# A decoder layer (mLSTM and SwiGLU) in float32: order of small steps at the seams between stages changed, on five engines

## The chip, the cores and the metric

One core of a Trainium2 chip runs the whole program. The metric is the device time of that core in microseconds. Its engines are TensorE (PE in the profile), VectorE (DVE), ScalarE (ACT), GpSimd (POOL) and SyncE (SP); each runs its own instruction list in order, and they meet only through semaphores.

## The reference

One layer over 2048 tokens of width 1024. The input is normalised, goes through a chunkwise mLSTM with 8 heads, is added back, normalised again, and goes through a gated feed-forward layer of width 2816:

```python
u = rmsnorm(h, mix_norm_g)
h = h + mlstm_mixer(u, w_in, b_if, norm_g, w_out)
u = rmsnorm(h, ffn_norm_g)
h = h + (jax.nn.silu(u @ w_gate) * (u @ w_up)) @ w_down
```

The mixer projects `u` to queries, keys, values, an output gate and two scalar gates per head; scans over chunks with a decayed state per head; normalises each head; multiplies with the sigmoid of the output gate; and projects with `w_out`.

## The kernel before

The tokens are done in two halves (`h` = 0, 1) of 1024, each half as 8 tiles (or chunks) of 128. Every large product is done as three passes of the matrix engine: each float32 operand is split into a high part, which ScalarE makes with a copy (`op_hi`, `proj_hi`, `feed_hi`, `drain_hi`), and a low part, which VectorE makes as the difference (`op_lo`, `proj_lo`, `feed_low`, `drain_lo`). The large products also use a seven-product (Strassen) scheme over 2x2 blocks, so that sums of blocks are needed: of the rows of `x` (`sum_early` on VectorE, `sum_late` with `sum_t3` and `sum_t4` on GpSimd) and of the weights (`proj_sums`, `feed_sums`, `drain_sum`).

A half goes through these stages:

1. Opening. `norm1_sum` (ScalarE) and `norm1_rows` (VectorE) normalise a tile of rows; TensorE transposes it (`turn_unit`, 16 units a stage), and the result is split (`op_hi`, `op_lo`). The units are transposed between the first projections (`project(n, k0, k1)`), each `project` needing its weights and, the first of them, the first four `op_lo`.
2. Projections, 84 units of 12 matmuls; the results are put together in `pkept` and stored (`store_block`, GpSimd). The last block but for one, `store_block(11, 1)`, waits for the last `sigmoid` on ScalarE.
3. Chunks `c` = 0 to 7: `spread`, `scores`, `weights`, `state_sums`, `outputs`, `turn_v`, `turn_heads`, and the output projection `out_tile(c, jj, k0, k1)` for the two halves `jj` of its columns, one chunk (`jj` = 0) or three (`jj` = 1) later. The values of a chunk lie in `v1[c % 2]`, whose last column holds ones; a memset on GpSimd writes it once per half, and `state_sums` waits for it through `ones_set`. `wo` is split into high and low parts in steps `split_out(jj, k)` on both engines. `add_out` adds an output tile into `res`, which a DMA has filled with rows of `x`.
4. The second turn: `norm2_sum`, `norm2_rows`, `sum_early(st + 1, p)`, `turn_unit(st + 1, n)`, between the last `out_tile` and the first `feed` units of the feed-forward layer. `feed` unit 0 waits for four `op_lo`.
5. `feed`, 11 groups of 14 units, then `drain`, 77 units `e` of 12 matmuls, which multiply with `w_down`. SyncE loads `g_in` for each `e` (four buffers) and, at the units in `LOAD_AT`, blocks of `w_down`. GpSimd loads `res` again, when the drains in `RES_AT` are done. In the last drains of the first half the opening of the second is begun: `ROWS_AT` and `SUMS_AT` say after which `e` a tile is normalised or summed, `TURN_AT` = 69 where four units are transposed.

The order on every engine is written out by hand, and an instruction that waits holds all behind it. The waits in `turn_unit` on `op_lo_done` say when a bank of PSUM is free again: unit `n` needs `op_lo` of unit `n - 2`, counted in order.

## Time and profile before

| | |
|---|---|
| median of 3 runs | 2154.61 us (2154.42 to 2155.74) |
| time of the profiled execution | 2154.42 us |
| its span in the trace | 2152.8 us |
| TensorE busy | 2121.9 us, 99% |
| VectorE busy | 1425.7 us, 66% |
| ScalarE busy | 939.2 us, 44% |
| GpSimd busy | 250.1 us, 12% |
| mean granted clock of TensorE | 0.999 |

The span goes from the first to the last record of the trace; the device time has 1.6 us around it. Lines such as L2139 are lines of the kernel; helpers such as `turn_four` (L1891) or `op_lo` (L1309) have one line for many places, so that a place is found by its time.

### The profile page before, as it was taken

To read this page: it belongs to the slowest core of one execution; us is meant where nothing else is said; L and a number is where in the kernel's file an instruction comes from. 1 tells how busy PE (TensorE), PEld (TensorE's weight loads), DVE (VectorE), ACT (ScalarE), POOL (GpSimd) and SP (SyncE) were. 2 spreads that over 40 slices of the span, in tenths; PEclk is the share of its full clock that TensorE was granted. 3 is DMA by queue.
4 is the path that set the end of the run, shared out by engine and by line. 5 is a ranking of instruction groups with operands and counts; after the bars stand their busy time and mean duration, and the time that the engine had idled before them with its cause. 6 is when DMAs were issued, how large, how long until landed. Compare 5 with 4: busy or idle time off the path is not lost.

```text
span 2152.8 us, 29471 instructions
## 1 busy us (share of the span) xinstructions
PE 2121.9 (99%) x10424; PEld 1762.6 (82%) x10440; DVE 1425.7 (66%) x2274; ACT 939.2 (44%) x1686; POOL 250.1 (12%) x357
## 2 busy tenths in 40 slices
PE   6999999999999999999999999999999999999999
PEld 5888888888888888888878888888888888888887
DVE  8765476787566565679677644767866657556764
ACT  5433674453333333345444347544533333334443
POOL 3211100021001010100121111001110101001000
PEclk9999999999999999999999999999999999999999
DMA  4333373223322334773414334632233232357443
GB/s 148 110 110 113 109 272 121 84 69 106 105 96 97 117 102 150 270 249 118 152 64 142 118 94 147 233 119 89 68 103 109 97 117 96 105 190 250 152 134 107
DMA packets 200288, 281.56 MB, mean 131 GB/s; under 512 B 12912, under 2 KB 131696, under 8 KB 200176
## 3 DMA queue, kind: packets, MB, share of 16 engines
q1 hardware_dynamic: 171696, 183.07, 26.5%
q0 software_dynamic: 28480, 97.02, 12.9%
q8 instruction: 68, 1.11, 0.2%
q14 instruction: 44, 0.36, 0.1%
HBM read 197.73 MB, written 82.31 MB: 130 GB/s over the span
## 4 chain that ended last, share of the span: by engine, by line
PE 94%; DVE 3%; DMA 1%; ACT 1%; issue 1%; POOL 0%; SPq 0%; DVEq 0%; POOLq 0%
PE ps L2247 13%; PE ps L2250 13%; PE ps L2249 13%; PE ps L1971 7%; PE ps L1975 7%; PE ps L1973 7%; PE ps L2295 6%; PE ps L2297 6%; PE ps L2299 6%; PE ps L1884 3%; PE ps L1886 3%; PE ps L1885 3%; PE ps L1891 2%; PE ps L2157 1%; DMA res<-in_x_dram 1%
## 5 line engine op out<-in xcount | busy, mean ns | idle before, releaser
L1722 DVE TENSOR_TENSOR ring<-raw_f,ring 128x512 fp32r<-128x512 f32 x308 | 211.4, 687 | 188.1 <-ACT ring L1148 186.6
L1148 ACT CAST ring<-raw_f 128x512 fp32r<-128x512 f32 x308 | 191.2, 623 | 208.7 <-PE ps L2250 193.2
L2247 PE MATMUL ps<-u_lo,ring 128*128 128x512 f32 x704 | 275.7, 392 | 0.0
L2250 PE MATMUL ps<-u_hi,ring 128*128 128x512 f32 x704 | 274.1, 389 | 0.0
L2249 PE MATMUL ps<-u_hi,ring 128*128 128x512 f32 x704 | 273.9, 389 | 0.0
L2295 PE MATMUL ps<-ring,ring 128*128 128x512 f32 x616 | 240.5, 390 | 2.0 <-DVE ring L1801 1.9
L2299 PE MATMUL ps<-ring,ring 128*128 128x512 f32 x616 | 239.7, 389 | 0.0
L2297 PE MATMUL ps<-ring,ring 128*128 128x512 f32 x616 | 239.7, 389 | 0.0
L2247 PE MATMUL ps<-t_op,ring 128*128 128x512 f32 x528 | 206.0, 390 | 0.0
L2250 PE MATMUL ps<-t_op,ring 128*128 128x512 f32 x528 | 205.5, 389 | 0.0
L2249 PE MATMUL ps<-t_op,ring 128*128 128x512 f32 x528 | 205.4, 389 | 0.0
L1190 ACT CAST ring<-g_in 128x512 fp32r<-128x512 f32 x154 | 95.6, 621 | 217.4 <-PE ps L2299 215.8
L1795 DVE TENSOR_TENSOR ring<-g_in,ring 128x512 fp32r<-128x512 f32 x154 | 106.3, 690 | 106.0 <-ACT ring L1190 106.0
L795 POOL DMA_DIRECT2D ops_hbm<-kept x154 | 83.6, 543 | 759.1 <-DVE kept L1820 559.6
L1321 DVE TENSOR_TENSOR pring<-raw,pring 128x512 fp32r<-128x512 f32 x132 | 90.7, 691 | 109.7 <-ACT pring L864 108.9
L1815 DVE TENSOR_TENSOR kept<-ps,kept 128x512 f32<-128x512 f32 x132 | 90.9, 689 | 105.7 <-PE ps L2250 105.7
L2250 PEld LDWEIGHTS ps<-u_hi,ring 128*128 128x128 f32 x704 | 132.1, 188 | 27.6
L2247 PEld LDWEIGHTS ps<-u_lo,ring 128*128 128x128 f32 x704 | 132.2, 188 | 27.1 <-issue 0.5
L2249 PEld LDWEIGHTS ps<-u_hi,ring 128*128 128x128 f32 x704 | 132.2, 188 | 26.9
L1971 PE MATMUL ps<-u_lo,pring 128*128 128x512 f32 x384 | 151.7, 395 | 2.4 <-DVE u_lo L1309 2.4
L1975 PE MATMUL ps<-u_hi,pring 128*128 128x512 f32 x384 | 150.3, 391 | 0.0
L1973 PE MATMUL ps<-u_hi,pring 128*128 128x512 f32 x384 | 150.3, 391 | 0.0
(223 smaller groups left out, 4180.3 us busy)
## 6 DMA issues: line engine op xcount, KB each, us to landing
ops_hbm<-kept POOLq DMA_DIRECT2D x154, 256.0 KB, 2.4
g_in<-ops_hbm SPq DMA_DIRECT2D x154, 256.0 KB, 2.7
raw<-in_ml_w_in_dram SPq DMA_DIRECT2D x24, 1024.0 KB, 5.4
proj_hbm<-pkept POOLq DMA_DIRECT2D x96, 256.0 KB, 2.7
raw_f<-in_ffn_w_gate_dram SPq DMA_DIRECT2D x44, 512.0 KB, 4.7
raw_f<-in_ffn_w_up_dram SPq DMA_DIRECT2D x44, 512.0 KB, 4.6
b<-in_ffn_w_down_dram SPq DMA_DIRECT2D x88, 256.0 KB, 4.6
x_in<-in_x_dram SPq DMA_DIRECT2D x16, 512.0 KB, 6.3
```

The source lines that it names most:

```text
L1148: nc.scalar.copy(four(ring[slot][:, 0, :]), feed_source(q, s)).then_inc(w_hi_done, 1)
L1722: nc.vector.tensor_tensor(four(ring[slot][:, 1, :]), feed_source(q, s), four(ring[slot][:, 0, :].bitcast(F32)), ALU.subtract).then_inc(w_l ...
L1795: nc.vector.tensor_tensor(ring[e % 3][:, 1, :], g_in[e % 4][:, :], ring[e % 3][:, 0, :].bitcast(F32), ALU.subtract).then_inc(ea_lo_done, 1)
L1971: pe.matmul(banks(bank), w[:, 0, now], moved(kind, 1, k), start=(fresh and k == 0), stop=False, skip_group_check=True)
L1973: pe.matmul(banks(bank), w[:, 0, now], moved(kind, 0, k), start=False, stop=False, skip_group_check=True)
L1975: last = pe.matmul(banks(bank), w[:, 1, now], moved(kind, 0, k), start=False, stop=(k == 3), skip_group_check=True)
L2247: pe.matmul(banks(bank), wh, moved(kind, 1, k), start=(fresh and k == 0), stop=False, skip_group_check=True)
L2249: pe.matmul(banks(bank), wh, moved(kind, 0, k), start=False, stop=False, skip_group_check=True)
L2250: last = pe.matmul(banks(bank), wl, moved(kind, 0, k), start=False, stop=(k == 3), skip_group_check=True)
L2295: pe.matmul(banks(bank + j), a[:, 0, now], w[:, 1, :], start=(fresh and n == 0), stop=False, skip_group_check=True)
L2297: pe.matmul(banks(bank + j), a[:, 0, now], w[:, 0, :], start=False, stop=False, skip_group_check=True)
L2299: last = pe.matmul(banks(bank + j), a[:, 1, now], w[:, 0, :], start=False, stop=(n == GROUPS - 1), skip_group_check=True)
```

## The change

Nothing is computed otherwise; instructions change their places and some waits their targets.

- Opening of the first half: in the lists of ScalarE and VectorE the first `op_hi` and `op_lo` come before the norm of tile 2, and so on; the norm of tile 4 comes before `op_lo(0, 3)`; `sum_early(0, 0)` comes after it; `add_unit(1, 1)` moves ahead of two `proj_sums`. TensorE transposes units 4 and 5 inside `project(0)`, not inside `project(1)`.
- GpSimd: the memset of the ones in `v1[1]` moves behind the loop with `store_block(11, 1)`.
- Chunks: `split_out(1, 3)` on VectorE moves from chunk 2 to the end of chunk 1; `out_tile` waits once for all eight parts of `wo`.
- Second turn: `out_tile(7, 1)` is cut at k=6; `sum_early(st + 1, 2)` and `op_lo` 3 change places with others; `feed_lo(0, 5)` comes before `op_lo(st + 1, 10)`.
- Drains: the loads of `LOAD_AT` and `RES_AT` come earlier; norm and sums of the next half get other units and stand before `op_lo` on VectorE.

```diff
--- before.py
+++ after.py
@@ -46,8 +46,8 @@
 NF = 14 * GROUPS
 RING = 7
 OP_UNITS = 16
-ROWS_AT = {36: 0, 39: 1, 42: 2, 46: 3, 50: 4, 54: 5, 58: 6, 73: 7}
-SUMS_AT = {52: 0, 71: 1, 72: 2, 75: 3}
+ROWS_AT = {36: 0, 39: 1, 42: 2, 46: 3, 50: 4, 54: 5, 58: 6, 71: 7}
+SUMS_AT = {52: 0, 72: 1, 74: 2, 75: 3}
 
 FIRST_UNITS = [("B", 0), ("C", 0), ("B", 1), ("B", 2), ("B", 3), ("A", 0), ("A", 1), ("A", 2), ("A", 3), ("C", 1),
                ("C", 2), ("C", 3)]
@@ -67,8 +67,7 @@
     ("B11", 0, 4, 2), ("B11", 4, 8, 2), ("B11", 8, 11, 4), ("B12", 0, 4, 6), ("B12", 4, 8, 6), ("B12", 8, 11, 10),
     ("B22", 0, 5, 4), ("B22", 5, 11, 8), ("B21", 0, 2, 8), ("B21", 10, 11, 10), ("B21", 2, 10, 12),
 )
-LOAD_AT = {6: 9, 7: 14, 8: 26, 9: 27, 10: 28}
-RES_AT = (0, 4, 11, 15)
+LOAD_AT = {6: 5, 7: 9, 8: 26, 9: 27, 10: 28}
 
 
 def down_load_of(kind, n):
@@ -744,9 +743,6 @@
                         pool.wait_ge(o_gated, done + 2)
                         store_block(g, 2)
                         for i, k in enumerate((1, 3) if g < PG - 1 else (3, 1)):
-                            if g == PG - 1 and k == 1:
-                                pool.wait_ge(p_stored[1], h * 368 + 368)
-                                nc.gpsimd.memset(v1[1][:, :, DV:VW], 1.0).then_inc(ones_set, 1)
                             pool.wait_ge(o_gated, done + 3 + i)
                             store_block(g, k)
                     else:
@@ -765,6 +761,8 @@
                                    x_rows[bass.ds(h * TILES + 2 * q, 2)].rearrange("t p d -> p t d"))\
                         .then_inc(res_loaded[q], 16)
 
+                pool.wait_ge(p_stored[1], h * 368 + 368)
+                nc.gpsimd.memset(v1[1][:, :, DV:VW], 1.0).then_inc(ones_set, 1)
                 pool.wait_ge(p_fed, h * PU + PU)
 
                 def store_h(i):
@@ -800,7 +798,7 @@
                 pool.wait_ge(ops_stored[0], h * 672 + 672)
                 pool.wait_ge(fed, h * NF + NF)
                 for q in range(4):
-                    pool.wait_ge(drained, past(h * NE + RES_AT[q]))
+                    pool.wait_ge(drained, past(h * NE + 3 * q))
                     pool.sem_inc(pool_passed, 1)
                     pool.dma_start(res[:, 2 * q:2 * q + 2, :],
                                    h_hbm[bass.ds(h * TILES + 2 * q, 2)].rearrange("t p d -> p t d"))\
@@ -928,12 +926,12 @@
                     nc.scalar.preload_act_table_set("natural_log_exp_and_others")
                     norm1_sum(0, 0)
                     norm1_sum(0, 1)
+                    op_hi(0, 0)
                     norm1_sum(0, 2)
-                    op_hi(0, 0)
+                    op_hi(0, 1)
                     norm1_sum(0, 3)
-                    op_hi(0, 1)
+                    op_hi(0, 2)
                     proj_hi(0, 0)
-                    op_hi(0, 2)
                     norm1_sum(0, 4)
                     op_hi(0, 3)
                     proj_hi(0, 1)
@@ -1458,19 +1456,19 @@
                 if h == 0:
                     norm1_rows(0, 0)
                     norm1_rows(0, 1)
+                    op_lo(0, 0)
                     norm1_rows(0, 2)
-                    op_lo(0, 0)
+                    op_lo(0, 1)
                     norm1_rows(0, 3)
-                    op_lo(0, 1)
+                    op_lo(0, 2)
                     proj_lo(0, 0)
-                    op_lo(0, 2)
+                    norm1_rows(0, 4)
                     op_lo(0, 3)
+                    sum_early(0, 0)
                     proj_lo(0, 1)
-                    norm1_rows(0, 4)
-                    sum_early(0, 0)
-                    proj_lo(0, 2)
                     norm1_rows(0, 5)
                     sum_early(0, 1)
+                    proj_lo(0, 2)
                     proj_lo(0, 3)
                     op_lo(0, 4)
                     norm1_rows(0, 6)
@@ -1481,11 +1479,11 @@
                     norm1_rows(0, 7)
                     op_lo(0, 6)
                     sum_early(0, 3)
+                    add_unit(1, 1)
                     proj_sums(0, 0, 0)
                     op_lo(0, 7)
                     proj_lo(0, 4)
                     op_lo(0, 8)
-                    add_unit(1, 1)
                     proj_sums(0, 1, 0)
                     op_lo(0, 9)
                 else:
@@ -1665,8 +1663,6 @@
                         weigh_queries(c)
                     weigh_keys(c)
                     weigh_scores(c)
-                    if c == 2:
-                        split_out(1, 3)
                     if c == 0:
                         for k in range(4, 8):
                             split_out(0, k)
@@ -1688,7 +1684,7 @@
                     if c:
                         add_out(c - 1, 0)
                     if c in (1, 2):
-                        for k in range(4 * c - 4, 4 * c - (c == 1)):
+                        for k in range(4 * c - 4, 4 * c):
                             split_out(1, k)
 
                 def feed_sums(n, q):
@@ -1740,10 +1736,10 @@
                 op_lo(st + 1, 0)
                 op_lo(st + 1, 1)
                 add_out(7, 0)
+                sum_early(st + 1, 2)
                 op_lo(st + 1, 2)
+                add_out(7, 1)
                 op_lo(st + 1, 3)
-                add_out(7, 1)
-                sum_early(st + 1, 2)
                 op_lo(st + 1, 4)
                 norm2_rows(7)
                 feed_low(0, 3)
@@ -1756,8 +1752,8 @@
                 feed_sums(0, 3)
                 op_lo(st + 1, 9)
                 feed_lo(0, 4)
+                feed_lo(0, 5)
                 op_lo(st + 1, 10)
-                feed_lo(0, 5)
                 op_lo(st + 1, 11)
                 feed_lo(0, 6)
 
@@ -1865,12 +1861,12 @@
                     if e >= GROUPS + 2 and (e - 2) % GROUPS == 0:
                         add_product(h, (e - 2) // GROUPS - 1)
                     if h + 1 < HALVES:
-                        if TURN_AT <= e < TURN_AT + 4:
-                            op_lo(2 * (h + 1), e - TURN_AT)
                         if e in ROWS_AT:
                             norm1_rows(h + 1, ROWS_AT[e])
                         if e in SUMS_AT:
                             sum_early(2 * (h + 1), SUMS_AT[e])
+                        if TURN_AT <= e < TURN_AT + 4:
+                            op_lo(2 * (h + 1), e - TURN_AT)
                 if h + 1 == HALVES:
                     add_product(h, 6)
 
@@ -2000,16 +1996,15 @@
                 project(0, 0, 2)
                 if h:
                     pe.wait_ge(added, past(h * 16 - 2))
-                    turn_unit(st, 4)
+                turn_unit(st, 4)
                 project(0, 2, 4)
                 if h:
                     pe.wait_ge(added, past(h * 16))
-                    turn_unit(st, 5)
+                turn_unit(st, 5)
                 project(1, 0, 2)
-                turn_unit(st, 6 if h else 4)
+                if h:
+                    turn_unit(st, 6)
                 project(1, 2, 4)
-                if h == 0:
-                    turn_unit(st, 5)
                 project(2, 0, 2)
                 if h == 0:
                     turn_unit(st, 6)
@@ -2169,9 +2164,9 @@
 
                     if k0 == 0:
                         pe.wait_ge(hglo_done, h * 8 + c + 1)
+                        pe.wait_ge(wolo_done, h * 16 + 8 * jj + 8)
                         if c:
                             pe.wait_ge(res_added, out_at(h, c - 1, jj))
-                    pe.wait_ge(wolo_done, h * 16 + 8 * jj + (4 if k1 <= 4 else 8))
                     last = three_passes(banks(jj), [(hg_hi[c % 3][:, k, :], hg_lo[c % 3][:, k, :], wo[jj][0][:, k, :],
                                                      wo[jj][1][:, k, :]) for k in range(k0, k1)], k0 == 0, k1 == KD)
                     if k1 == KD:
@@ -2218,9 +2213,9 @@
                 pe.wait_ge(hg_done, h * 8 + 8)
                 turn_unit(st + 1, 2)
                 out_tile(7, 0, 0, KD)
-                out_tile(7, 1, 0, 4)
+                out_tile(7, 1, 0, 6)
                 turn_unit(st + 1, 3)
-                out_tile(7, 1, 4, KD)
+                out_tile(7, 1, 6, KD)
                 turn_unit(st + 1, 4)
 
                 def feed(n, q, b, k0=0, k1=4):
```

## Rows read from the trace of the kernel before

**Rows 1.** the page, part 1: busy us, share of the span, instructions

```profile
PE 2121.9 (99%) x10424; PEld 1762.6 (82%) x10440; DVE 1425.7 (66%) x2274; ACT 939.2 (44%) x1686; POOL 250.1 (12%) x357
```

**Rows 2.** what TensorE waited for: us in total, times, longest

```profile
PE ps L1891 <- DVE x_in L1285: 9.8, 2, 9.1
```

**Rows 3.** timeline by start, first half, chunk 1: start us, us, what, [idle before]

```profile
285.88 0.11 POOL L749 MEMSET v<- 128x8 f32 x1 [2.00 <-DMA proj_hbm<-pkept]
...
293.43 1.10 PE L2139 MATMUL ps<-v,kw 128*64 128x129 f32 x16
...
293.69 0.63 ACT L1003 ACTIVATE pkept<-pkept 128x512 f32<-128x512 f32 x1
...
294.89 0.75 POOL L732 DMA_DIRECT2D proj_hbm<-pkept  x1 [8.90 <-ACT pkept L1003]
...
296.30 1.23 DVE L1596 TENSOR_TENSOR hg_lo<-og,hg_hi 128x1024 fp32r<-128x1024 f32 x1 [1.11 <-ACT hg_hi L1102]
```

**Rows 4.** timeline, first half, end of chunk 1 and chunk 2

```profile
305.36 0.69 DVE L1651 TENSOR_TENSOR res<-ps,res 128x512 f32<-128x512 f32 x1 [0.68 <-DMA res<-in_x_dram]
...
305.97 2.07 DVE L1528 SCALAR_TENSOR_TENSOR wo<-wo_raw,head_g,wo 128x512 fp32r<-128x512 f32 x3
...
309.45 1.10 PE L2139 MATMUL ps<-v,kw 128*64 128x129 f32 x16 [0.86 <-DVE kw L1575]
...
313.34 1.23 DVE L1596 TENSOR_TENSOR hg_lo<-og,hg_hi 128x1024 fp32r<-128x1024 f32 x1 [1.11 <-ACT hg_hi L1102]
...
314.62 0.50 PE L1884 MATMUL ps<-wo,hg_hi 128*128 128x512 f32 x1
```

**Rows 5.** timeline, second half, the same place

```profile
1368.85 0.69 DVE L1651 TENSOR_TENSOR res<-ps,res 128x512 f32<-128x512 f32 x1 [1.56 <-DMA res<-in_x_dram]
...
1372.94 1.10 PE L2139 MATMUL ps<-v,kw 128*64 128x129 f32 x16 [1.74 <-DVE kw L1575]
```

**Rows 6.** timeline, first half, chunk 3

```profile
322.03 2.73 DVE L1528 SCALAR_TENSOR_TENSOR wo<-wo_raw,head_g,wo 128x512 fp32r<-128x512 f32 x4
...
323.53 0.48 PE L1884 MATMUL ps<-wo,hg_hi 128*128 128x512 f32 x1
```

**Rows 7.** timeline, first half, second turn and first feed

```profile
444.65 2.35 DVE L1309 TENSOR_TENSOR u_lo<-ps,u_hi 128x1024 fp32r<-128x1024 f32 x2
...
447.12 0.69 DVE L1651 TENSOR_TENSOR res<-ps,res 128x512 f32<-128x512 f32 x1
...
447.65 0.48 PE L2247 MATMUL ps<-u_lo,ring 128*128 128x512 f32 x1
...
454.66 1.09 PE L1891 MATMUL ps<-ident,res 128*128 128x128 f32 x8 [0.89 <-DVE u_lo L1309]
...
464.48 1.23 DVE L1309 TENSOR_TENSOR u_lo<-ps,u_hi 128x1024 fp32r<-128x1024 f32 x1
...
466.20 0.60 PE L1891 MATMUL ps<-ident,res 128*128 128x128 f32 x4
```

**Rows 8.** timeline, end of the first half's drain

```profile
1075.19 0.68 DVE L1302 TENSOR_TENSOR x_in<-x_in,x_in 128x512 f32<-128x512 f32 x1
...
1077.86 0.50 PE L2295 MATMUL ps<-ring,ring 128*128 128x512 f32 x1 [1.24 <-DVE ring L1801]
```

**Rows 9.** timeline, opening of the first half

```profile
22.11 0.79 PE L1971 MATMUL ps<-u_lo,pring 128*128 128x512 f32 x1 [2.36 <-DVE u_lo L1309]
...
31.55 1.78 DVE L1321 TENSOR_TENSOR pring<-raw_first,pring 128x512 fp32r<-128x512 f32 x1
...
34.52 0.66 PE L1891 MATMUL ps<-ident,t_home 128*128 128x128 f32 x4 [1.75 <-DVE t_op L1309]
...
47.03 0.93 PE L1891 MATMUL ps<-ident,t_rows 128*128 128x128 f32 x4 [1.26 <-DVE t_op L1309]
```

**Rows 10.** windows: stretch, us, busy of each engine, granted clock (PEclk), DMA share, GB/s

```profile
48.00:50.00 2.00, 2.00 (x7) 1.45 (x6) 1.97 (x4) 1.01 (x1) 0.00 (x0) 0.50 0.00 0
```

**Rows 11.** windows of the first drains: the same columns

```profile
950.00:960.00 10.00, 10.00 (x45) 8.28 (x45) 6.79 (x11) 4.57 (x8) 0.00 (x0) 1.00 1.01 390
```

## The prediction

> **What bounds the kernel now.** The page comes first: TensorE is busy 2121.9 of 2152.8 us [rows 1]. So nothing done faster on another engine shortens the run except where TensorE waits, and there are only 31 us of that. The list of what TensorE waited for comes next; its largest entry is the wait for the first normalised tile, 9.8 us [rows 2], which the change leaves alone. The remaining 21 us are small waits at seams between stages, where VectorE or a hand-written order decides. So the time is found in the timeline around each seam the diff touches: for every edit I ask whether TensorE stands there now, and whether it will stand there afterwards. I replay each seam with the durations of its rows. Matmuls 128x512 start 0.2275 us apart, a `turn_unit` of eight transposes takes 0.8 to 0.9 us.
>
> **The ones column, `v1[1]` (GpSimd), first half.** Now GpSimd writes the ones at 285.88, and TensorE starts `state_sums(1)`, which waits for them (`ones_set` at 2), at 293.43 [rows 3]. The change puts that memset behind `store_block(11, 1)`. This store waits for the last sigmoid, whose last exponential runs from 293.69 for 0.63; GpSimd issues the store at 294.89 and spends 0.75 on it [rows 3]. So the memset runs from 295.64 to 295.75, and `state_sums(1)` starts at about 295.8: 2.4 us late. Nothing else can be run by TensorE meanwhile; its order is written out. Behind it are `outputs(1)`, `turn_v(2)`, `out_tile(0, 0)` and everything after, and ScalarE and VectorE wait for the sums of chunk 1, so the whole chunk moves by 2.4. The load of `res` behind the memset moves by 0.1 only.
>
> **What is absorbed, and `split_out(1, 3)`.** In the first half VectorE adds `out_tile(0, 0)` into `res` at 305.36, held 0.68 by the DMA of `res` [rows 4]. Later by 2.4 through its own chain (hrow would end at 307.1), it finds the data there; that hides 0.7. But four instead of three `split_out` follow (3 in 2.07, so 0.66 more, rows 4), and the keys `kw` behind them come 2.3 late: `state_sums(2)` moves from 309.45 to 311.7, +2.3. The split taken out of chunk 2 (0.66 until the next instruction) brings `hg_low(1)` forward. It now ends at 314.57, and `out_tile(1, 0)` starts at 314.62 [rows 4], about 0.35 after its turn has come; this is won back, +1.9. Next, `out_tile(0, 1)` used to ask for `wo` k 0 to 3 and now asks for all eight. It starts at 323.53, but the four last splits run from 322.03 for 2.73, to 324.76 [rows 6]. VectorE's side moves by +1.6 (2.3 less 0.66) to 326.4, TensorE arrives at 325.45: another 1.0. First half: +2.9.
>
> Second half: the same, but the DMA holds VectorE for 1.56 at 1368.85, and TensorE then waits 1.74 for `kw` [rows 5]. The chain of VectorE would come at 1369.6 with the delay, so only 0.75 + 0.66 = 1.4 gets through; less 0.35, plus 1.0: +2.0.
>
> **Second turn (`out_tile(7, 1)`, `sum_early(st+1, 2)`), both halves.** The split of `out_tile` at k=6 only moves `turn_unit(3)` by 1.4 us; its work is the same. But VectorE now does `sum_early(2)` (two instructions, next one after 1.33) before `op_lo(2)`, and `add_out(7, 1)` before `op_lo(3)`. `op_lo(2)` and `(3)` now run from 444.65 and `feed` begins at 447.65, directly behind the transposes; `add_out(7, 1)` is at 447.12 [rows 7]. `feed` waits for four `op_lo`. Replayed: `sum_early(2)` 444.65, `op_lo(2)` 445.98 to 447.2, `add_out` still 447.12 because TensorE ends `out_tile(7, 1)` at 447.0, `op_lo(3)` 447.72 to 448.94: `feed` starts at 449.0, +1.35. In return the 0.89 us wait before the transposes at 454.66 goes, and 0.2 behind it; left +0.25. Then `feed_lo(0, 5)` before `op_lo(10)`: it is two instructions, 1.2 us, so `op_lo(10)` goes from 464.48 to 465.8 and ends at 467.0. The transposes at 466.20 wait for it and arrive at 466.45: +0.6. Per half +0.85, together +1.7.
>
> **Drain tail.** `drain` 72 waits 1.24 us for VectorE, which does `sum_early(1)` at 1075.19 and its second instruction first [rows 8]. With the sum behind `drain_lo(72)` but `norm1_rows(1, 7)` (2.1) before `op_lo(2)`, which had idle time ahead of it, `drain(72)` starts at 1077.1 instead of 1077.86: -0.7. `drain(73)` waits about as before; `drain(74)` gains 0.2 more, since the norm of tile 7 is done. -0.95. ScalarE's share, 1.6 us, ends just before `op_hi(2)` has its transposes.
>
> **Opening.** In the new order VectorE normalises tile 4 (1.9 us) before `op_lo(0, 3)`, and ScalarE's later `norm1_sum(0, 2)` makes tiles 2 and 3 0.8 to 1.0 late. `project(0)` begins at 23.8 instead of 22.11 [rows 9]. Yet the transposes of `turn_unit(6)` at 34.52 had waited 1.75, for `op_lo(4)` behind a `proj_lo` that took 1.77 instead of 0.68 while GpSimd was summing [rows 9]. In the new order `sum_early(0, 0)` is 0.9 earlier, one `proj_lo` (0.6) more lies before `op_lo(4)`: it ends at 34.1, TensorE arrives at 34.4 with the same work done. So the late start costs nothing. From there VectorE's chain is 0.35 ahead, and the transposes at 47.03, which waited 1.26 for it [rows 9], come 0.3 earlier: -0.3. Just there the clock was granted at 0.50 (level 1.2 GHz) for 48 to 50 us [rows 10], after TensorE had stood idle twice; I leave it in. If it stayed at 2.4 GHz, 1.9 us would be won; if the late start were not absorbed, +1.8.
>
> A `proj_lo` that stretched to 1.77 beside GpSimd's sum [rows 9] raises the question whether the moved memset can be held up in the same way; in rows 3 the store ahead of it takes 0.75 and ends before VectorE's next instruction on two SBUF tiles, so the rows give +2.4. The Trainium skill ("SBUF — State Buffer", section "SBUF: two separate sides") says that VectorE and GpSimd lock a common port pair for a whole instruction, and that GpSimd can't write a DMA's descriptors while VectorE holds it. By that rule the trace's 1.77 is such a lock; if it struck here too, the sum below would be 3.6 higher. It speaks against the change, and is a rival.
>
> **Loads.** `RES_AT` and `LOAD_AT` bring 3 MB of `res` and 2.8 MB of weights forward by 5 to 16 us in the first ten drains. A `g_in` block is issued some 11 us before ScalarE needs it. At the rate of up to 390 GB/s [rows 11], the largest backlog I can construct (2.6 MB at 889 us) takes 7 us: 0, hidden by that lead; if not hidden, up to 3 us per half. Nothing is gained, since TensorE doesn't wait there.
>
> **Sum.** +2.9 + 2.0 + 1.7 - 0.95 - 0.3 = +5.3 us on the profiled execution, 2154.42 us (1.6 more than its span). The median of the runs is 2154.61, so 2159.9.
>
> **Rivals.**
> Opening rescues it (not slower): the waits of 1.75 and 1.26 and the half clock (1.9) all go, for a start 1.8 late: -3.1 instead of -0.3. It decides as soon as more than 1 us beyond the forecast is won there. For it: all three stand in rows 9 and 10. Against: VectorE has no gap there. 2157.1.
> The memset costs nothing: the wait for ones is not last, say because the last sigmoid comes early. The other edits then leave 0.66 - 0.35 + 1.0 = 1.3 per half: 2157.6. Against: `state_sums(1)` starts 1.5 us before the store is even issued.
> The port holds the ones: the memset or the store is held until VectorE's `hg_low(0)`, which reads two SBUF tiles from 296.30 to 297.53 [rows 3], has ended; 1.8 us more each half, 2163.5. Against: by the rows the memset is over at 295.75. This is the case that the skill's rule would make.
> Starved drains: `g_in` comes late at 890 and in the second half, 2 to 3 us each: 2165. Against: the lead of 11 us.
> Faster by 0.2%: would need every wait at the seams to go and no new one; no mechanism for it.
>
> **How the numbers follow.** A measurement here tells 0.2% (4.3 us, above 2158.9 us) from no change. Chances: forecast 0.60, opening 0.12, memset free 0.12, port 0.06, drains 0.06, faster 0.04. The forecast's own range is 2157.8 to 2162.3 from the bounds of the second turn (0 to +2.0 per half), tail (-1.9 to +0.7) and opening; about 0.08 of its 0.60 lies below 2158.9. Slower 0.52 + 0.12 = 0.64, same 0.08 + 0.24 = 0.32, faster 0.04. For 8 in 10 the range reaches from below the opening's case to above the port's: 2155.8 to 2164.0.
>
> **What would show it.** In the profile after: TensorE waits about 2.4 us before `state_sums(1)` in each half, released by the memset of `v1[1]`; about 1 us before the first `out_tile(0, 1)` and 1.3 before the first `feed`, released by VectorE; the wait of 0.89 at 454.66 gone; `drain(72)`'s wait near 0.5. The first `project` is 1.7 late, and its lateness is gone ten us later. A granted clock of 1.00 all through the opening, or no wait before `state_sums(1)`, would prove the sum wrong.

## The result, and the profile after

| | us |
|---|---|
| after, median of 5 runs | 2167.71 (2164.3 to 2168.82) |
| before, median of 5 runs in the same comparison | 2155.17 (2154.42 to 2155.88) |
| ratio after / before | 1.0056, 95% interval 1.0041 to 1.0072 |
| predicted | 2159.9 (2155.8 to 2164.0) |
| profiled execution after: time, span | 2168.73, 2167.0 |

The change makes the kernel slower, as forecast, but by 12.5 us, where 5.3 were forecast, and outside the range. Three more executions of it are on record, at 2162.66, 2168.73 (the profiled one) and 2172.47 us, so that its times spread over 10 us.

The first part of the page of the kernel after, to be read against [rows 1]: TensorE is busy for 4.7 us more. The program has the same matmuls in both (the 16 by which the pages differ, 10424 and 10440, are `mask,ident_b` matmuls that the trace of before has no record of). It is a first hint that more than waiting is in it.

```profile
PE 2126.6 (98%) x10440; PEld 1767.5 (82%) x10440; DVE 1424.0 (66%) x2274; ACT 939.5 (43%) x1686; POOL 249.3 (12%) x357
```

What TensorE waited for in the kernel after, from 280 to 440 us (all of the chunks of the first half; columns: total, times, longest):

```profile
PE ps L2134 <- issue: 2.4, 1, 2.4
PE ps L2159 <- DVE pkept L1454: 1.0, 1, 1.0
PE ps L1880 <- DVE wo L1526: 0.9, 1, 0.9
PE ps L2134 <- DVE kw L1573: 0.8, 1, 0.8
```

These are the predicted waits: 2.4 before `state_sums(1)`, 0.9 (1.0 predicted) for `wo` before the first `out_tile(0, 1)`. The one for `kw`, 0.8, is about as long as before. The first is put down to "issue", because the profile sees no releaser; the timeline of the same place shows it:

```profile
292.81 0.63 ACT L1001 ACTIVATE pkept<-pkept 128x512 f32<-128x512 f32 x1
...
294.00 0.75 POOL L731 DMA_DIRECT2D proj_hbm<-pkept  x1 [11.01 <-ACT pkept L1001]
...
294.75 0.13 POOL L765 MEMSET v<- 128x8 f32 x1
...
294.98 1.99 PE L2134 MATMUL ps<-v,kw 128*64 128x129 f32 x16 [2.36 <-issue]
...
296.89 2.09 PE L2148 MATMUL ps<-state,qw 64*128 64x129 f32 x16
```

Exponential, store, memset, `state_sums(1)`: the chain of [rows 3], in the predicted order. What was not predicted stands in the second column. `state_sums` takes 1.99 us; a chunk later, behind a wait of only 0.77, it takes its usual 1.10:

```profile
313.44 1.10 PE L2134 MATMUL ps<-v,kw 128*64 128x129 f32 x16 [0.77 <-DVE kw L1573]
```

The windows say why. Columns: stretch, length, busy time and count of PE, PEld, DVE, ACT, POOL, granted clock, DMA share, GB/s. First the kernel before, then after:

```profile
294.00:300.00 6.00, 6.00 (x58) 5.39 (x55) 4.08 (x10) 3.34 (x5) 1.67 (x3) 1.00 1.00 352
```

```profile
292.00:294.00 2.00, 0.61 (x6) 0.37 (x4) 2.00 (x3) 1.37 (x3) 0.00 (x0) 0.91 1.03 388
294.00:300.00 6.00, 5.03 (x37) 4.49 (x38) 1.53 (x2) 1.04 (x1) 1.50 (x3) 0.50 1.04 356
300.00:302.00 2.00, 2.00 (x18) 2.00 (x18) 0.26 (x1) 0.22 (x1) 0.00 (x0) 0.88 1.02 405
1362.00:1368.00 6.00, 4.71 (x35) 4.18 (x36) 1.85 (x2) 1.04 (x1) 1.49 (x3) 0.50 1.04 362
```

While TensorE stands idle for the ones, its granted clock falls to 0.50 (the level 1.2 GHz), and it stays there for 6.83 us by the trace's record of the clock, from 293.6 and again, in the second half, from 1362.0. In 6 us, the first of which is still wait, 37 matmuls start instead of 58. Of the first 6.83 us, 1.3 lie in the wait itself, up to 294.98, where nothing is lost; the other 5.5 at half speed lose 2.7 us of work. `state_sums(2)` comes 4.9 us later against its surroundings in the first half, where 2.3 were predicted, and 4.0 in the second, where 1.4 were predicted: 2.6 more each time [rows 4, 5]. The Trainium skill ("TensorE: Matmul & The Clock Gate", section "HAM oscillation — how this bites in real kernels") describes a kernel that lets TensorE idle between its matmuls and pays for the slow clock again after each such gap. The gaps of its example are longer than the 2.36 us here. The trace shows the same price behind the shorter gap, 1.99 against 1.10 us for the same `state_sums`; the table further down shows that it isn't paid behind every gap.

The other missing part lies in the drains of the second half. The timeline of TensorE and ScalarE there, and the windows:

```profile
1976.96 0.39 PE L2294 MATMUL ps<-ring,ring 128*128 128x512 f32 x1
...
1977.66 0.62 ACT L1188 CAST ring<-g_in 128x512 fp32r<-128x512 f32 x1 [7.24 <-DMA g_in<-ops_hbm]
...
1979.66 0.67 PE L2290 MATMUL ps<-ring,ring 128*128 128x512 f32 x1 [2.31 <-DVE ring L1797]
```

```profile
1970.00:1980.00 10.00, 7.69 (x34) 6.10 (x33) 3.52 (x6) 2.76 (x6) 0.71 (x1) 0.99 1.04 390
1980.00:1984.00 4.00, 4.00 (x12) 3.10 (x12) 3.82 (x7) 0.88 (x2) 0.00 (x0) 0.60 0.74 205
```

ScalarE waits 7.24 us for `g_in`, TensorE 2.31 for what follows from it, and behind that the clock falls again, for 3.41 us. The DMA engines are busy to 1.04 from 1970 to 1980, where the kernel before has 0.75. How long a `g_in` takes from its issue to its landing is the last line of the view of this tile, first of the kernel before (1926 to 1971 us), then after (1940 to 1985):

```profile
DMA to landing us min/median/max: 2.4/3.5/9.0
```

```profile
DMA to landing us min/median/max: 2.6/4.0/13.7
```

By estimate from the 0.2275 us between matmuls, the four buffers give a lead of four units of 12 matmuls, 4 x 2.73 = 10.9 us, the "some 11 us" of the prediction. Before, the slowest block lands within it; after, it lands 2.8 us beyond it, and TensorE waits 2.31. A small stall of the same kind is in the first half: the matmul at 909.32 starts 0.46 late.

Where the 14.2 us between the two spans lie, by the starts of the same instructions in the two traces:

| stretch | predicted | trace | difference |
|---|---|---|---|
| opening | -0.3 | -0.9 | -0.6 |
| chunks, first half | +2.9 | +5.6 | +2.7 (clock) |
| second turn, first half | +0.85 | +0.8 | 0 |
| drains up to 1060 | 0 | +0.5 | +0.5 (late `g_in`) |
| drain tail | -0.95 | -1.1 | -0.15 |
| chunks, second half | +2.0 | +4.7 | +2.7 (clock) |
| second turn, second half | +0.85 | +0.8 | 0 |
| drains from 1560 | 0 | +3.9 | +3.9 (late `g_in` 2.5, clock) |

Take out the clock, for which the sum had no term, and the late `g_in`, which it put at 0, and every term but the opening's is right within 0.15 us. The opening is -0.9 for another reason than stated: the transposes at 47.03 start at 47.02, their wait is the same, and instead of the fall of the clock at 47 us [rows 10] there is none. The windows of the kernel after, against 0.50 in [rows 10]:

```profile
48.00:50.00 2.00, 1.36 (x7) 1.05 (x6) 1.97 (x4) 1.01 (x1) 0.00 (x0) 1.00 0.00 0
```

All traces together say what this is worth. Where no fall is at 47 us, `state_sums(0)` of the first half starts at 279.36 to 279.55 with the old opening (six traces) and at 279.45 to 279.76 with the new one (five traces; a sixth, e6, has 278.98, with another record of the clock before 27 us); where there is one, it starts at 280.3 to 281.2 with either. The new opening wins nothing; the -0.9 is the fall that the profiled execution of before happened to have.

### The profile page after: what moved, and what is told of

It is laid out like the page before. It is cut to its first block, busy times and chain, and to the rows that moved or that the text cites. A ratio compares the mean times of both kernels' runs of the same rounds, so it can differ in the third digit from the quotient of the medians.

```text
span 2167.0 us, 29487 instructions
## 1 busy us (share of the span) xinstructions
PE 2126.6 (98%) x10440; PEld 1767.5 (82%) x10440; DVE 1424.0 (66%) x2274; ACT 939.5 (43%) x1686; POOL 249.3 (12%) x357
## 4 chain that ended last, share of the span: by engine, by line
PE 90%; DVE 5%; DMA 1%; ACT 1%; issue 1%; SPq 0%; DVEq 0%; ACTq 0%
PE ps L2242 13%; PE ps L2245 13%; PE ps L2244 13%; PE ps L1967 7%; PE ps L1969 7%; PE ps L1971 7%; PE ps L2290 6%; PE ps L2292 6%; PE ps L2294 6%; PE ps L1880 2%; PE ps L1882 2%; PE ps L1881 2%; PE ps L1887 1%; PE ps L2152 1%; DMA g_in<-ops_hbm 1%
```

## The experiments

Each time stands beside that of the kernel before on the same chip in the same series: 2154.47 in the first series (e1 to e4), 2154.40 in the second (e5 to e8), 2155.62 in the third (e9 to e12) and 2155.55 in the last (e13 to e16). "The changed kernel" is 2167.71, measured beside 2155.17. The same kernel before thus moves by 1.2 us from series to series; a difference between runs of two series is uncertain by about that much, and where it matters, the difference of their distances from the kernel before is given too.

### The ones and the clock

**e1, the changed kernel, memset back in its place**

```diff
+                            if g == PG - 1 and k == 1:
+                                pool.wait_ge(p_stored[1], h * 368 + 368)
+                                nc.gpsimd.memset(v1[1][:, :, DV:VW], 1.0).then_inc(ones_set, 1)
...
-                pool.wait_ge(p_stored[1], h * 368 + 368)
-                nc.gpsimd.memset(v1[1][:, :, DV:VW], 1.0).then_inc(ones_set, 1)
```

> The changed kernel with one thing put back: the memset of the ones in v1[1] stands again ahead of store_block(11, 1). Clock theory: the 2.4 us wait before state_sums(1) also brings TensorE's granted clock to the 1.2 GHz level for 6.8 us, in both halves, so that the edit costs 1.7 + 0.75 of waiting that gets through plus 2 x 2.6 = 7.7 us against the kernel before. With the memset back both falls of the clock are gone: about 8 us faster than the changed kernel (2159.5). Rival, waits alone: the fall of the clock has another cause (the second wait, the denser order around it) and stays; then only the waits go, 3 us less, 2164.5.

Measured: 2161.5 us (2160.81 to 2165.74), ratio 1.0038 (1.0024 to 1.0051). 6.2 less than the changed kernel (5.5 against the kernel before of each), nearer to the 8 of the clock theory than to the 3 of waits alone, but not all of it. In the profiled execution (span 2159.2, 7.8 less) both falls at `state_sums(1)` are gone. The waits from 280 to 440 us show what came in their place:

```profile
PE ps L2135 <- DVE kw L1574: 2.8, 1, 2.8
PE ps L2160 <- DVE pkept L1455: 1.0, 1, 1.0
PE ps L1881 <- DVE wo L1527: 0.7, 1, 0.7
```

Without the late ones, VectorE gets to `add_out(0, 0)` early and stands before the DMA of `res` for 1.93 us (0.68 in [rows 4]); the four splits follow, the wait for `kw` becomes 2.8 us, and there the clock fell, for 3.41 us. Here the edits hide each other: the wait for the ones is gone, and a longer one for `kw` takes its place.

**e2, the kernel before, memset late; e3, the same, filled.** e2 is the edit of e1 the other way round on the kernel before. e3 adds, ahead of the wait for the ones, matmuls whose results nothing uses:

```diff
+                    if c == 1:
+                        for _ in range(10):
+                            pe.matmul(banks(1), ident_b[:, :], mask[:, :, :].rearrange("p a t -> p (a t)"),
+                                      start=True, stop=True, skip_group_check=True)
                     pe.wait_ge(ones_set, h * 2 + (1 if c == 0 else 2))
```

> The kernel before with this one edit alone: the memset behind store_block(11, 1). Clock theory: TensorE waits 2.4 us before state_sums(1) and then runs 6.8 us at 1.2 GHz, twice; +1.7 + 0.75 + 2 x 2.6 = +7.7 us, 2162.5 to 2163. Waits alone: the same waits, clock at 1.00, +2.5 us, 2157.6.

> As the run with the late memset alone, but TensorE is given 10 matmuls 128x512 (bf16, results overwritten, 2.3 us) ahead of its wait for the ones, so that it stands idle for only some 0.1 us at this place although state_sums(1) starts as late. This separates the wait from the idleness. Clock theory: the clock stays at 1.00 and the kernel is 2.5 to 3 us slower than before (2158). If instead lateness itself cost the 7.7 (through the other engines and the DMA), it would be as slow as the run without the filling, 2162.5 to 2163.

Measured: e2 2160.16 us (2159.07 to 2160.79), ratio 1.0024 (1.0015 to 1.0033); e3 2156.07 us (2155.8 to 2157.48), ratio 1.0005 (0.9996 to 1.0014). The timeline of e3:

```profile
292.32 2.32 PE L2134 MATMUL ps<-mask,ident_b 128*128 128x512 bf16 x10
...
294.62 0.13 POOL L766 MEMSET v<- 128x8 f32 x1
...
294.80 1.10 PE L2142 MATMUL ps<-v,kw 128*64 128x129 f32 x16 [0.16 <-POOL v L766]
```

and the windows, first of e2, then of e3:

```profile
294.00:300.00 6.00, 4.96 (x37) 4.43 (x37) 1.59 (x2) 1.05 (x1) 1.50 (x3) 0.50 1.04 359
1362.00:1368.00 6.00, 6.00 (x53) 5.43 (x54) 1.48 (x2) 0.58 (x2) 0.48 (x1) 0.72 1.03 372
```

```profile
294.00:300.00 6.00, 5.84 (x61) 4.96 (x60) 2.38 (x6) 1.86 (x2) 1.38 (x3) 1.00 1.03 349
1362.00:1368.00 6.00, 6.00 (x38) 5.33 (x37) 3.39 (x11) 3.30 (x5) 0.71 (x1) 1.00 1.04 411
```

This is the cleanest pair of the study. `state_sums(1)` starts just as late in both, at the memset; all that differs is that TensorE has something to do meanwhile. The clock stays at 1.00, `state_sums` takes 1.10 again, and 4.1 of the 5.7 us are gone. So of the edit's 5.7 us in the medians, 1.6 are lateness and 4.1 are clock. In the profiled executions `state_sums(3)` comes later against `state_sums(0)` of its half by 1.67 and 0.70 us in e3 and by 4.27 and 2.31 in e2 than before: 2.4 of lateness, as predicted (2.5), and 4.2 of clock. The medians show less lateness; the fall at 47 us, worth 1.0 us in the profiled execution of before and absent in those of e2 and e3, may be part of that. e2 is below the 7.7 expected; in its profiled execution the second fall lasted 3.41 us, and not 6.83.

**e4, the kernel before, memset waits for a later step of ScalarE**

```diff
                                 pool.wait_ge(p_stored[1], h * 368 + 368)
+                                pool.wait_ge(o_step, h * 28 + 26)
                                 nc.gpsimd.memset(v1[1][:, :, DV:VW], 1.0).then_inc(ones_set, 1)
```

> The kernel before, with the memset in its place but made to wait for the same step of ScalarE that the second last store waits for, so that TensorE's wait before state_sums(1) is only some 0.6 to 1.7 us, not 2.4. Clock theory with a price per fall: either no fall (then +0.3 to +1.3 us, 2156) or, if already this short a wait brings the clock down, +2.6 x 2 more, 2161. It tells whether the length of the wait matters. Waits alone: +0.3 to +1.3.

Measured: 2155.03 us (2154.16 to 2156.88), ratio 1.0001 (0.9992 to 1.001). The edit didn't produce the short wait: in the trace `state_sums(1)` doesn't wait at all, since that step came early enough. It says nothing on short waits for the ones. It did show something else: TensorE waits 2.0 us for `kw` in both halves, and the clock fell behind the second of these waits (3.41 us, from 1375) and not behind the first.

**e8 and e9, the changed kernel, filled.** The edit of e3, in e8 on the changed kernel, in e9 on the changed kernel with `LOAD_AT` and `RES_AT` put back (as e6, below).

> The changed kernel with 10 matmuls 128x512 ahead of the wait for the ones, so that TensorE stands idle only 0.1 us at that place, and every other instruction comes as late as in the changed kernel. Clock theory: both falls of the clock at state_sums(1) are gone, 2 x 2.6 = 5.2 us faster than the changed kernel, 2162.5, and the wait for kw behind it grows by the time that the slow clock had hidden. If the falls had another cause: 2167.5.

> The changed kernel with LOAD_AT and RES_AT put back and the 10 matmuls ahead of the wait for the ones: the filling once more, with no stalls of the drains to blur it. Against the changed kernel with the loads put back alone, which took 2163.14 us. Clock theory: the two falls of 6.83 us at half clock are gone and nothing else changes, 2 x 3.4 = 6.8 us of lost clock less what the slow stretch had hidden of the wait for kw: 5 to 5.5 us faster, 2158. Rival: the filling brings nothing in the changed kernel (as its first trial seemed to say, 2167.34 against 2167.71): 2163.

Measured: e8 2167.34 us (2163.49 to 2169.45), only 0.4 less than the changed kernel, against the clock theory's 5.2; e9 2158.69 us (2158.16 to 2160.56), ratio 1.0017 (1.0008 to 1.0026), 4.4 less than the 2163.14 of e6, or 5.7 less when each is taken against the kernel before of its series; 5 to 5.5 were expected. In the profiled execution of e8 both falls at the ones are gone. But the drains of the first half had a longer stall than in any other trace:

```profile
PE ps L2294 <- DVE ring L1797: 3.5, 1, 3.5
```

```profile
910.00:916.00 6.00, 5.84 (x15) 4.59 (x16) 4.32 (x8) 1.64 (x4) 0.00 (x0) 0.53 0.50 152
```

3.5 us of wait and 6.83 us of half clock, where the changed kernel had lost 0.5: in this execution the drains took back what the chunks had won. ScalarE had waited 8.44 us for a `g_in` there, whose slowest landing took 15.5 us. In e9, without the early loads, nothing stalls there, and the filling is worth about what was expected. Whether the earlier arrival of the work makes the congestion of the drains worse, or e8's five executions fell badly (they lie from 2163.5 to 2169.5), was not told apart.

### The loads of the drains

**e5, the kernel before with the new loads; e6, the changed kernel with the old ones**

```diff
-LOAD_AT = {6: 9, 7: 14, 8: 26, 9: 27, 10: 28}
-RES_AT = (0, 4, 11, 15)
+LOAD_AT = {6: 5, 7: 9, 8: 26, 9: 27, 10: 28}
+RES_AT = (0, 3, 6, 9)
```

> The kernel before with the new LOAD_AT and RES_AT alone. Congestion theory: with the loads of w_down and res 5 to 16 us earlier, g_in blocks land later (up to some 14 us after their issue, where they took at most 9), ScalarE's drain_hi comes too late for TensorE near 890 to 910 us and again near 1965 to 1985 us, with a fall of the clock behind the longer stall: +0.5 to +4.5 us, not the same in each execution. Rival, hidden: the lead of g_in covers it and the 3 us in the changed kernel came from the shift of everything ahead; then no stall here, 2154.5.

> The changed kernel with LOAD_AT and RES_AT put back. Congestion theory: no wait before a drain in the first ten units of either half and no fall of the clock near 1980 us: 3 to 4.6 us faster than the changed kernel, 2163.5 to 2164.5, with less spread between executions. Hidden: the stalls stay, 2167.

Measured: e5 2160.35 us (2155.0 to 2162.44), ratio 1.0023 (1.0014 to 1.0032): +5.9. e6 2163.14 us (2162.31 to 2163.78), ratio 1.0039 (1.0026 to 1.0053): 4.6 less than the changed kernel (3.8 against the kernel before of each), and its executions lie within 1.5 us, where those of the changed kernel lie 4.5 apart. In the traces, TensorE's waits in the drains: e5 1.3 and 2.4 us, e6 none. The waits of ScalarE from 1945 to 1985 us in e5:

```profile
ACT ring L1190 <- PE ps L2299: 17.7, 11, 1.9
ACT ring L1190 <- DMA g_in<-ops_hbm: 7.3, 1, 7.3
```

The profiled execution of e5 was a lighter one (2158.28, no fall of the clock); the heavier ones, up to 2162.4, have no trace.

**e13 and e14, the kernel before with the new `RES_AT` alone, and with the new `LOAD_AT` alone**

> The kernel before with the new RES_AT alone (the four 1 MB loads of res at drains 0, 3, 6, 9 instead of 0, 4, 11, 15). The two sets together cost 5.4 us. If it is the res loads that crowd out g_in: all of that, +4 to +6, with a wait of ScalarE for g_in of over 5 us. If both have to come together: under +1.5 in each of the two runs.

> The kernel before with the new LOAD_AT alone (blocks of w_down at units 5 and 9 instead of 9 and 14). SyncE issues these loads in the same queue as g_in, so that a g_in block can stand behind them: if that is the cause, +4 to +6. If it is the sum of all bytes in the stretch: some +1 here, some +1 with res alone, 5.4 together.

Measured: e13 2156.15 us (2153.57 to 2157.09), ratio 1.0 (0.9991 to 1.0009); e14 2155.29 us (2153.28 to 2157.26), ratio 0.9997 (0.9988 to 1.0006). Each alone costs nothing that can be told from zero (the intervals reach 2 us to either side); together they cost 5.9. The traces show how. Between 880 and 930 us ScalarE waits for `g_in` not at all before, 2.2 us in e13, 4.3 in e14 and 6.2 in e5, and the slowest `g_in` issued from 860 to 915 lands after 8.0, 9.6, 11.4 and 13.4 us. In the second half (1945 to 1985) the wait is 1.6 before, none in e13, 4.4 in e14 and 7.3 in e5. TensorE waited in e5 alone. So the lead of `g_in`, 10.9 us, is a stock: either edit uses up part of it, and only both use more than there is. Loads of `res` come from GpSimd's queue and those of `w_down` from SyncE's, and they add up all the same. The Trainium skill ("DMA: Bandwidth & Descriptors", section "Issuing engines are not separate DMA queues") says so: transfers issued by several engines run interleaved on the same 16 DMA engines. These three runs fit it; they don't show where the transfers meet.

### The second turn, `wo`, the opening

**e7, the changed kernel, second turn put back**

```diff
-                sum_early(st + 1, 2)
                 op_lo(st + 1, 2)
-                add_out(7, 1)
                 op_lo(st + 1, 3)
+                add_out(7, 1)
+                sum_early(st + 1, 2)
```

(and the cut of `out_tile(7, 1)` at k=4, `feed_lo(0, 5)` behind `op_lo(st + 1, 10)`)

> The changed kernel with the second turn put back (out_tile(7, 1) cut at k=4, sum_early(st + 1, 2) behind add_out(7, 1), op_lo(st + 1, 10) ahead of feed_lo(0, 5)). By the term of the prediction: 0.85 us less per half, 1.7 us faster than the changed kernel, 2165.5 to 2166; the first feed waits for nothing and the wait of 0.9 before the transposes is back. If a second turn edit costs nothing: 2167.5.

Measured: 2165.85 us (2162.39 to 2168.46), ratio 1.005 (1.0036 to 1.0064): 1.9 less (1.1 against the kernel before of each), where 1.7 were expected; the spread of the executions is larger than the difference, so that it is the traces that carry it. TensorE's waits from 440 to 480 us, in the changed kernel and in e7:

```profile
PE ps L2242 <- DVE u_lo L1307: 1.1, 1, 1.1
PE ps L1887 <- DVE u_lo L1307: 0.6, 1, 0.6
```

```profile
PE ps L1887 <- DVE u_lo L1307: 0.9, 1, 0.9
```

1.7 against 0.9, 0.8 us a half; from 1500 to 1560 us the lists are the same.

**e10, the kernel before with the edits around `wo` alone**

```diff
-                    if c == 2:
-                        split_out(1, 3)
...
-                        for k in range(4 * c - 4, 4 * c - (c == 1)):
+                        for k in range(4 * c - 4, 4 * c):
...
+                        pe.wait_ge(wolo_done, h * 16 + 8 * jj + 8)
...
-                    pe.wait_ge(wolo_done, h * 16 + 8 * jj + (4 if k1 <= 4 else 8))
```

> The kernel before with the edits around wo alone: split_out(1, 3) in chunk 1 and one wait for all eight parts in out_tile. The terms of the prediction: +0.66 for kw before state_sums(2), -0.35 at out_tile(1, 0), +1.0 before the first out_tile(0, 1), in each half: +2.6 us, 2157. Rival: with the wait for kw at 1.6 and 2.4 us instead of 0.9 and 1.7 the clock falls there too, 1.7 us a time: 2159 to 2160.

Measured: 2158.38 us (2155.48 to 2161.28), ratio 1.0016 (1.0007 to 1.0025): +2.8, by the terms +2.6, and below the 2159 to 2160 of the rival. But the executions are 5.8 us apart, and the profiled one is the fastest of them, without any fall of the clock.

**e16, the kernel before with a swap in chunk 1; e15, the same swap and the `wo` edits.** VectorE does the splits of `wo` before `add_out(0, 0)` and not behind it:

```diff
-                    if c:
+                    if c > 1:
                         add_out(c - 1, 0)
                     if c in (1, 2):
                         for k in range(4 * c - 4, 4 * c - (c == 1)):
                             split_out(1, k)
+                    if c == 1:
+                        add_out(0, 0)
```

> The kernel before with the wo edits (which alone cost 2.8 us in the median, 0 to 6 in single executions) and with VectorE's splits of chunk 1 ahead of add_out(0, 0). The splits then fill VectorE's wait for the DMA of res. Fall theory: the wo edits cost more than their terms because the wait for kw, longer by 0.66 and by what the DMA adds, brings the clock down in some executions; without the DMA in the chain the wait is under 1 us, the spread between executions goes, and what is left is the 0.9 before the first out_tile(0, 1) in each half less the 0.9 and 1.7 of kw waits that the swap saves: 2153 to 2154. Rival: the wait for wo itself is what costs; then 2156 and the same spread.

> The kernel before with the swap in chunk 1 alone (three split_out(1, k) ahead of add_out(0, 0)). The wait of state_sums(2) for kw, 0.9 us in the first half and 1.7 in the second, is gone: 2.6 us less, and more where an execution had a fall of the clock behind it; 2151.5 to 2152.5 against 2154.6 to 2155.6 before. If most of the 4.1 us that it brought on top of the opening edits came with them: 0 to -1.

Measured: e16 2151.27 us (2150.99 to 2152.13), ratio 0.9978 (0.9969 to 0.9987): 4.3 less than before. e15 2154.17 us (2153.87 to 2155.61), ratio 0.9992 (0.9983 to 1.0001). Both lie within 1.8 us, where the kernel before itself lay between 2154.19 and 2158.09 in that series. In e16 the wait for `kw` is gone; this is all that TensorE waited for from 1340 to 1500 us:

```profile
PE ps L2166 <- DVE pkept L1456: 1.0, 1, 1.0
```

The two waits for `kw` in the profiled execution of before, 0.9 and 1.7 [rows 4, 5], are 2.6, and the spans differ by 2.5. The other 1.7 of the 4.3 in the medians would fit falls of the clock behind longer waits for `kw` in the executions of before that were not profiled; that is argued, not shown. e15 against e16 gives the price of the `wo` edits without the DMA's wait, 2.9 us. The waits of e15 from 1340 to 1500:

```profile
PE ps L2164 <- DVE pkept L1456: 1.0, 1, 1.0
PE ps L1884 <- DVE wo L1528: 0.9, 1, 0.9
PE ps L2139 <- DVE kw L1575: 0.7, 1, 0.7
```

The first is in e16 too. The other two, 0.9 + 0.7, less the 0.35 that was predicted to be won back, are 1.25, and 2.5 for both halves. The fall theory had 2153 to 2154 and a narrow spread; the median is 0.2 above that and the spread came out. Whether the spread is gone because the falls of the clock are, or because the time no longer hangs on a DMA, these runs don't tell apart.

**e11, the kernel before with the edits of opening and drain tail alone; e12, the same with the swap**

> The kernel before with the edits of the opening and of the drain tail alone. By the landmarks of the changed kernel's trace: gates(1) 0.9 us earlier (of which up to 1.7 belong to the half clock at 47 us, which does not come in each execution), tail 1.1 us less: -1.1 to -2.0, 2152.5 to 2153.3. Rival, absorbed: what the opening wins is lost again at the first add_out, which waits for the DMA of res in any case; then -1.1 from the tail alone or less, 2153.5 to 2154.4.

> As the run with opening and tail alone, and in chunk 1 VectorE does its three split_out(1, k) before add_out(0, 0) instead of behind it, so that the time in which it waits for the DMA of res (0.68 us in the first half, 1.56 in the second, more when it comes earlier) is filled with work it has to do anyway. If this wait is what holds kw and state_sums(2): 0.7 + 1.6 us less than the run without it, 2150.5 to 2151. If kw is bound by something else (the scores of TensorE): no difference.

Measured: e11 2154.0 us (2152.64 to 2154.57), ratio 0.9993 (0.9984 to 1.0002), -1.6; e12 2149.89 us (2149.43 to 2151.64), ratio 0.9975 (0.9965 to 0.9985). e11 can't be told from no change for certain; it lies near the tail's measured 1.1, and the traces give the opening nothing. e12 is 4.1 below e11, where 2.3 were expected, much as the swap alone won 4.3 in e16. It is the fastest version of the study: 5.7 us less than the kernel before, and 17.8 less than the changed kernel.

### Waits and falls of the clock

All waits of TensorE of 1.5 us and more in the chunks and drains of the profiled executions, and how long the clock stood at 1.2 GHz with them or behind them:

| wait | in | us | half clock, us |
|---|---|---|---|
| ones | after | 2.4, 2.4 | 6.8, 6.8 |
| ones | e2 | 2.4, 2.4 | 6.8, 3.4 |
| ones | e6 | 2.4, 2.4 | 6.8, 6.8 |
| ones | e7 | 2.4, 2.4 | 3.4, 6.8 |
| `kw` | e1 | 2.8, 1.8 | 3.4, none |
| `kw` | e14 | 1.8, 2.1 | 3.4, 3.4 |
| `kw` | e4 | 2.0, 2.0 | none, 3.4 |
| `kw` | e13 | 1.8, 1.8 | none |
| `kw` | before, e5, e10 | 1.7; 1.9; 1.5, 1.7 | none |
| `g_in` | after, e7 | 2.3; 2.0 | 3.4; 3.4 |
| `g_in` | e8 | 3.5, 2.2 | 6.8, 3.4 |
| `g_in` | e5 | 2.4 | none |

The kernels without such a wait (e3, e9, e11, e12, e15, e16) have no fall in these stretches. In the opening a shorter wait is enough at times: the fall from 47.3 us in before [rows 10] comes behind a wait of 1.26 us, with one of 0.45 us 2.3 us ahead of it.

The same wait of 1.8 us brought a fall in one execution and none in another (310 to 314 us in e14, then in e13, which had the same code up to there):

```profile
310.00:314.00 4.00, 4.00 (x35) 3.59 (x31) 2.89 (x4) 1.69 (x3) 0.00 (x0) 0.59 0.03 8
```

```profile
310.00:314.00 4.00, 4.00 (x47) 3.70 (x44) 2.89 (x4) 1.75 (x3) 0.00 (x0) 1.00 0.03 9
```

## Why the prediction was right or wrong

**The ones: the step that failed.** The step was right in all that it said: the chain of exponential, store and memset, the place, 2.4 us. Wrong was that the sum ended there. "`state_sums(1)` starts at about 295.8: 2.4 us late" prices a wait of TensorE at its length, and the clock behind it at nothing, without a reason. It also costs the speed of the matmuls behind it, about 2.7 us each time here; e2 and e3 measured it, 5.7 for the late memset with the idleness and 1.6 without it. It is the largest term that was missed, some 5.4 us in the profiled execution. The profile of before had a hint of it: the prediction reads a granted clock of 0.50 from 48 to 50 us "after TensorE had stood idle twice" [rows 10], asks whether this fall would go, and doesn't ask whether the new idle time would bring others. No rival stood for it either.

**The loads: the second step that failed.** "0, hidden by that lead; if not hidden, up to 3 us per half" chose the wrong end; the case was named as a rival (starved drains, 2165), with 0.06 of the chance. The backlog of 7 us was set against the lead of 11 us as if the whole lead were free. Before, the slowest `g_in` already took 9.0 us to land, which left 2; after, it took 13.7. e13 and e14 show why a look at each load in turn can't find it; each alone is free, and both together are not. Measured: 3.8 to 5.9 us in the medians, 4.4 in the profiled execution, falls of the clock included.

**`split_out`, `wo`.** +0.66 at `kw`, +1.0 at `out_tile(0, 1)` (0.88 and 0.9 measured): right, 2.6 predicted for both halves, 2.8 (e10) and 2.9 (e15 against e16) measured.

**Second turn.** +1.35 at the first `feed` and +0.85 in all: +1.35 and +0.8 in the traces, 1.9 for both halves in e7. **Drain tail:** -0.95, -1.1 in the trace; `drain(72)` still waits 0.52, where 0.5 was predicted.

**Opening.** The prediction said that "a granted clock of 1.00 all through the opening" would prove the sum wrong, and this sign came: in the trace after, the clock is at 1.00 from 27.4 us on, at 47 us too. The first `project` is 2.0 late (1.7 predicted) and its lateness is gone at 34.50; that VectorE is 0.3 ahead from there on was wrong, since the transposes at 47.03 moved by 0.01 only. The 0.9 in the profiled execution hang on the fall of the clock there, which comes and goes between executions of the same code (it is in e16 and e4, not in e2 and e3; with the new opening in e9 and e11, not in e12). So the term is 0, and that it came out with the right sign is luck. One row is misread by a hair: `proj_lo` at 31.55 took 1.78, not 1.77 [rows 9].

**The port.** The memset starts at the end of the store's 0.75 us and takes 0.13; nothing was held, and the rival didn't come. The section of the Trainium skill that the prediction names ("SBUF — State Buffer", "SBUF: two separate sides") has a condition that the prediction leaves out: a VectorE instruction with two SBUF inputs is in conflict only with a GpSimd instruction that reads SBUF, and the memset's row shows no input. Yet VectorE had no instruction running from 294.31 to 295.42, so that no run here shows what would happen beside one.

**The order of the edits.** The terms add up less well than they look. From the kernel before, ones (5.7), loads (5.9), `wo` (2.8), second turn (1.9, from e7) and opening with tail (-1.6) give 14.7, where 12.5 were measured. Part of it is that the late ones cover the wait for `res` that the others run into; e1 shows a wait for `kw` of 2.8 us coming out behind it. The rest is within what the series and the spread of the executions leave open.

## What to carry to other kernels

A wait of the engine that bounds the kernel has two prices, its length and the slower matmuls behind it; where the profile shows one fall of the clock after an idle stretch, a new wait of about two microseconds has to be priced with the chance of another, and if it can't be avoided, something for TensorE to do in it wins most of it back (4.1 of 5.7 us here). Loads that are brought forward draw on the same lead of the stream that must not starve: try them together, and look at the spread between executions as well as the median. And an instruction that waits for a DMA should stand behind the work that doesn't; moving three splits ahead of one `add_out` was worth 4.3 us, more than any edit of the change won.

## What the runs showed of the hardware that was not expected

- The granted clock fell for 3.41 or 6.83 us at a time with waits of 1.8 to 3.5 us in the chunks and drains, either within the wait (at 293.6, in a wait from 292.6 to 295.0) or up to 1.2 us after its end (at 310.7 in e14, behind a wait that ended at 309.5), and not always: 1.8, 2.0 and 2.4 us were seen with a fall and without one.
- Ten bf16 matmuls without any use, 2.32 us of them, kept it at 1.00 in both halves of e3.
- The time of one and the same kernel is uneven: executions of e10, whose wait for `kw` hangs on a DMA, are 5.8 us apart, and those of e16, which doesn't have this wait, 1.1 us; that falls of the clock make up the difference is argued from the table and not shown, since each kernel has one trace.
- Two sets of loads that cost nothing measurable each (ratios 1.0 and 0.9997) cost 5.9 us together: the slowest `g_in` lands after 9.6 or 11.4 us with one of them and after 13.4 with both, and the lead is 10.9.
